# Expert stage of a two-layer decoder step: token rows stand still in four column groups, weights move

## What is computed

```python
g_sel = jnp.argmax(g_logit, axis=-1)                 # 1 group of 4
top_p, top_i = lax.top_k(jax.nn.softmax(e_logit, axis=-1), TOP_K)   # 2 experts of 8 in it
...
def expert_block(args):
    xb, e = args
    hid = jax.nn.silu(xb @ w_eg[e]) * (xb @ w_eu[e])   # 1024 -> 256, twice
    return hid @ w_ed[e]                               # 256 -> 1024
...
y = jnp.einsum('nkd,nk->nd', y_slot, gates)
```

## Time and profile before

| | us |
|---|---|
| median of three runs | 2886.36 |
| lowest, highest of the three | 2873.0, 2890.05 |
| span of the profiled execution | 2865.1 |
| expert blocks, first layer: first matmul to last | 1019.97 to 1387.8 |
| TensorE busy | 2605.3 (91%) |
| DMA over the span | 135 GB/s mean |

### The profile page before, as it was taken

One profiled execution on the slowest core, in us unless ns is written; L12 is line 12 of the kernel. 1 busy time (PEld: TensorE's weight loads), 2 busy tenths in 40 slices (PEclk: granted clock), 3 DMA queues, 4 the chain that ended last, 5 costly groups with the idle time before them and its releaser, 6 DMA issues.

```text
span 2865.1 us, 38998 instructions
## 1 busy us (share of the span) xinstructions
PE 2605.3 (91%) x15964; PEld 1817.8 (63%) x15964; DVE 1176.1 (41%) x2208; ACT 720.4 (25%) x1448; POOL 413.7 (14%) x561
## 2 busy tenths in 40 slices
PE   7999988899999889999699999888899997999994
PEld 5645556556667578887465455565666765888872
DVE  4155557543223433233351555584323334333225
ACT  1124453331003301111311244443211222111113
POOL 0004225110000011111100123251000000111111
PEclk9999998898999989999799999989999997999996
DMA  4001001342141268898410100113223214888954
GB/s 162 17 17 32 5 5 34 115 184 74 37 163 68 105 233 324 321 339 329 180 54 4 38 11 8 34 39 151 111 89 127 82 45 175 294 330 329 331 205 184
DMA packets 76932, 385.65 MB, mean 135 GB/s; under 512 B 25086, under 2 KB 31868, under 8 KB 65724
## 3 DMA queue, kind: packets, MB, share of 16 engines
q1 hardware_dynamic: 53164, 304.90, 29.2%
q0 software_dynamic: 23040, 76.59, 7.6%
q10 hardware_dynamic: 576, 2.10, 0.2%
HBM read 355.55 MB, written 44.55 MB: 140 GB/s over the span
## 4 chain that ended last, share of the span: by engine, by line
PE 73%; DVE 10%; PEld 4%; ACT 4%; issue 4%; DMA 2%; POOLq 1%; POOL 1%; PEldq 1%; SPq 0%; DVEq 0%; ACTq 0%
PE ps L1319 16%; PE ps L667 12%; PE ps L1332 8%; PE ps L1237 4%; PE ps L725 4%; PE ps L805 4%; PEld ps L667 4%; PE ps L817 2%; PE ps L833 2%; PE ps L1003 2%; PE ps L1308 2%; PE ps L783 2%; DVE arena L1993 1%; DVE nmax L1894 1%; PE ps L936 1%
## 5 line engine op out<-in xcount | busy, mean ns | idle before, releaser
L667 PE MATMUL ps<-arena,ring 128*128 128x352 f32 x1704 | 508.4, 461 | 3.4 <-DVE arena L1783 2.4
L1319 PEld LDWEIGHTS ps<-arena 128*128 128x128 f32 x4096 | 470.8, 193 | 35.7 <-issue 35.7
L1319 PE MATMUL ps<-arena 128*128 128x104 f32 x4096 | 470.5, 276 | 4.9 <-issue 2.5
L667 PEld LDWEIGHTS ps<-arena,ring 128*128 128x128 f32 x1704 | 324.8, 191 | 184.9 <-issue 5.7
L1332 PE MATMUL ps<-arena 128*104 128x512 f32 x512 | 230.4, 593 | 2.6 <-ACT arena L1713 2.6
L1713 ACT ACTIVATE arena<-ps 104x1024 f32<-104x1024 f32 x64 | 65.5, 1023 | 470.7 <-PE ps L1332 470.7
L2419 DVE TENSOR_SCALAR arena<-arena 128x208 f32<-128x208 f32 x64 | 17.2, 269 | 401.2 <-ACT arena L1706 401.2
L2554 POOL DMA_INDIRECT arena<-xrow,arena x64 | 70.5, 1102 | 671.7 <-PE ps L1308 353.9
L1332 PEld LDWEIGHTS ps<-arena 128*104 128x104 f32 x512 | 81.9, 170 | 104.0 <-issue 104.0
L805 PE MATMUL ps<-arena 96*128 96x512 f32 (+3 forms) x384 | 147.1, 493 | 0.0
L1481 ACT ACTIVATE ring<-ps 128x512 f32<-128x512 f32 (+2 forms) x192 | 87.3, 490 | 127.2 <-PE ps L817 127.1
(11 more groups left out here) (411 smaller groups left out, 3587.5 us busy)
## 6 DMA issues: line engine op xcount, KB each, us to landing
arena<-in_w_e SPq DMA_DIRECT2D x64, 3072.0 KB, 13.5
ring<-in_ring SPq DMA_DIRECT2D x56, 512.0 KB, 3.6
arena<-yrow SPq DMA_DIRECT2D x16, 1024.0 KB, 7.7
arena<-in_mem_k SPq DMA_DIRECT2D x16, 512.0 KB, 7.1
arena<-in_mem_v SPq DMA_DIRECT2D x16, 512.0 KB, 10.4
xrow<-arena SPq DMA_DIRECT2D x16, 512.0 KB, 6.3
x<-in_x SPq DMA_DIRECT2D x3, 1408.0 KB, 11.5
out_y<-arena SPq DMA_DIRECT2D x3, 1408.0 KB, 5.6
```

Source lines behind the costliest of these rows:

```text
L667: mm = pe.matmul(ps[:, (j % 2) * NCH + c, 0:CH], ring[:, j // per, (j % per) * units + k, :], src[:, k, tok], start=k == k0, stop=k == uni ...
L1319: mm = pe.matmul((gate_ps if m < 2 else up_ps)[:, m % 2, 0:rows], w_e[j][:, at:at + P], xb_t[:, p, k, 0:rows], start=k == 0, stop=k == KT - 1)
```

## The change

All of it concerns the expert stage.

1. A block has 128 rows and no longer belongs to one expert. `CAP` is 96 rows (three groups of 32), so 32 experts x 96 rows fill `NB` = 24 blocks. Each 32-row group of a block has its own expert: block 0 has experts 0, 0, 0, 1; block 1 has 1, 1, 2, 2; block 2 has 2, 3, 3, 3; and so on with a period of three blocks and four experts.
2. `gate_up` takes the rows as stationary operand, 32 at a time, and moves 512 weight columns (gate and up together) past them; the four groups write four 32-partition strips of one PSUM bank. It waits for the weights of *all* experts of its block before its first matmul.
3. The hidden values now come out with the row on the partition. A new step `turn_h` (two transposes) and a new copy by ScalarE, `keep_h`, turn them for `down`. `down` uses four 32-row groups as well.
4. `hidden` works on 128x256 in one bank of PSUM, after `take_x` of the next block instead of before it.
5. The weight slots are still four. Expert `e` is loaded when `down` of the last block that uses expert `e - 4` is over.
6. Loops are written out: 24 blocks, and up to `OVER` = 24 overflow blocks, each behind its own `If`, instead of a hardware loop over four.

```diff
-CAP = 104
-OVER = 20
-NBLK = NE + OVER
+CAP = 96
+GRP = 32
+NB = NE * CAP // P
+OVER = 24
+NBLK = NB + OVER
...
+        def experts_of(n):
+            return [(n * P + GRP * g) // CAP for g in range(P // GRP)]
+        def last_block(e):
+            return (CAP * (e + 1) - 1) // P
...
-                        sp.wait_ge(dn_done, n + 1)
-                        sp.sem_inc(turn, 1)
-                        load_w(j, n + 4)
+                for e in range(4, NE):
+                    sp.wait_ge(dn_done, last_block(e - 4) + 1)
+                    load_w(e % 4, e)
...
-                    pe.wait_ge(we_full[j], full)
+                    for e in sorted(set(experts)):
+                        pe.wait_ge(we_full[e % 4], 16 * loads(e))
                     pe.wait_ge(tx_evac, n + 1)
-                    pe.wait_ge(h_ready, n)
-                    for m in range(4):
-                        for k in range(KT):
-                            at = k * 512 + m * P
-                            mm = pe.matmul((gate_ps if m < 2 else up_ps)[:, m % 2, 0:rows], w_e[j][:, at:at + P], xb_t[:, p, k, 0:rows],
-                                           start=k == 0, stop=k == KT - 1)
+                    if n >= 2:
+                        pe.wait_ge(h_ready, n - 1)
+                    for k in range(KT):
+                        for g, e in enumerate(experts):
+                            r = slice(GRP * g, GRP * (g + 1))
+                            mm = pe.matmul(ps[r, 2 + n % 2, :], xb_t[:, n % 2, k, r], w_e[e % 4][:, k * 512:(k + 1) * 512],
+                                           start=k == 0, stop=k == KT - 1, skip_group_check=True)
...
+                def turn_h(n):
+                    pe.wait_ge(h_ready, n + 1)
+                    if n >= 1:
+                        pe.wait_ge(ht_evac, n)
+                    for m in range(2):
+                        mm = pe.transpose(ps[:, 6, m * P:(m + 1) * P], h_e[:, n % 2, m * P:(m + 1) * P], ident)
+                    mm.then_inc(ht_done, 1)
...
+                            for g, e in enumerate(experts):
+                                r = slice(GRP * g, GRP * (g + 1))
+                                mm = pe.matmul(ps[r, 4 + f, :], h_t[:, k, r], w_e[e % 4][:, at:at + 512],
+                                               start=k == 0, stop=k == 1, skip_group_check=True)
...
+                turn_x(0)
+                for n in range(NB):
+                    gate_up(n, experts_of(n), loads_of)
+                    if n >= 1:
+                        turn_h(n - 1)
+                    if n + 1 < NB:
+                        turn_x(n + 1)
+                    if n >= 1:
+                        down(n - 1, experts_of(n - 1))
+                turn_h(NB - 1)
+                down(NB - 1, experts_of(NB - 1))
...
+                    for o in range(OVER):
+                        with pe.If(n_over > o):
+                            n, experts = NB + o, [o % 4] * (P // GRP)
...
+                def keep_h(n):
+                    act.wait_ge(ht_done, n + 1)
+                    act.activation(h_t.rearrange("p m t -> p (m t)"), ps[:, 6, 0:2 * P], ACT.Copy).then_inc(ht_evac, 1)
...
+                take_x(0)
+                for n in range(NB):
+                    if n + 1 < NB:
+                        take_x(n + 1)
+                    hidden(n)
```

More of the change, by code:

```diff
@@ L1333, in down @@
                     mm.then_inc(dn_done, 1)
[L1335 to L1348, removed]
@@ L1349, in _, with loads_of @@
-                for n in range(NE - 3, NE):
-                    block(n, n % 4, n // 4, (n + 1) % 4, (n + 1) // 4, more=n < NE - 1)
-                down(NE - 1, 1, 3)
+                def loads_of(e):
+                    return e // 4 + 1
+                turn_x(0)
[5 more added lines that the diff above has]
+                        turn_x(n + 1)
+                    if n >= 1:
+                        down(n - 1, experts_of(n - 1))
@@ L1352, in _ @@
+                turn_h(NB - 1)
+                down(NB - 1, experts_of(NB - 1))
                 n_over = pe.value_load(over_i[0:1, 0:1], min_val=0, max_val=OVER)
                 with pe.If(n_over > 0):
[L1354 to L1360, removed]
+                    for o in range(OVER):
+                        with pe.If(n_over > o):
+                            n, experts = NB + o, [o % 4] * (P // GRP)
+                            turn_x(n)
+                            gate_up(n, experts, lambda e: NE // 4 + o // 4 + 1)
+                            turn_h(n)
+                            down(n, experts)
@@ L1718, in _ @@
[L1718 to L1723, removed]
-                    gate_exp(n)
-                    keep_y(n - 1, (n - 1) % 2)
-                keep_y(NE - 1, 1)
-                act.wait_ge(y_out, NE)
+                for n in range(NB):
+                    gate_exp(n)
+                    if n >= 1:
+                        keep_h(n - 1)
+                        keep_y(n - 1)
@@ L1728, in _ @@
+                keep_h(NB - 1)
+                keep_y(NB - 1)
+                act.wait_ge(y_out, NB)
                 n_over = act.value_load(over_i[0:1, 0:1], min_val=0, max_val=OVER)
                 with act.If(n_over > 0):
[L1730 to L1737, removed]
+                    for o in range(OVER):
+                        with act.If(n_over > o):
+                            n = NB + o
+                            gate_exp(n)
+                            keep_h(n)
+                            keep_y(n)
+                            act.wait_ge(y_out, n + 3)
+                            act.sem_inc(turn, 1)
@@ L2362, in _ @@
                 step(dve.tensor_tensor(jump, oend, nov, ALU.subtract))
[L2363 to L2364 removed]
+                step(dve.tensor_scalar(jump, jump, float(P), float(P * NB - CAP), ALU.mult, ALU.add))
+                step(dve.tensor_tensor(jump, jump, base, ALU.subtract))
                 dve.wait_ge(ranked, 2)
@@ L2574, in _ @@
                 stage_end(pool, 9)
-                for n in range(NE):
-                    if n + 2 < NE:
+                for n in range(NB):
+                    if n + 2 < NB:
                         pool.wait_ge(tx_done, n + 1)
```

116 lines of the change are left out of this document (48 added, 68 removed).

## The result

The changed kernel takes 3191.45 us (median of four runs; the kernel before 2887.11 beside it): 1.108 times the time before, 95% interval 1.105 to 1.112.

A forecast was written before the change was run, and what follows sets the result against it. TensorE was taken to bound the kernel, with late weights stalling it after the change. Span 2865.1 + 279 (expert stages) + 33 (overflow block) + 15 (jumps) = 3192, plus 21.3 to the median: 3213 us, range 3110 to 3330.

The forecast's parts named there:

- TensorE bounds the stage and DMA is close behind: Expert stages before the change: TensorE busy 100.00 of 100 us, 11.27 us an expert; DMA engines at 0.91.
- rival 4: Expert stage: weights are there in time, the DMA engines bound the stage, 2852 us; chance 3%.
- Four groups side by side: `gate_up` and `down`: four 32-column groups share the array; 7.0 and 3.5 us, a block of 128 rows 11.9 us.
- Which blocks stall: Expert stage: blocks 3, 4, 6, 7, ... 21, 22 wait for a weight load's whole landing, 14 a layer.
- What a stall costs: Each wait for weights in the expert stage: landing 12.0 us, issue 0.4, low clock 2.3, together 14.7 us.
- Until the last regular `down`: Expert stage up to its last regular `down`: 139.5 us more a layer, 279 for both.
- Overflow: End of the first layer's expert stage: one expert with 100 rows makes one overflow block, about 33 us.
- Jumps: The other 23 overflow bodies, jumped over by every engine: some 0.7 us each on TensorE, 15 us taken in all.
- The sum: Whole kernel's span: 2865.1 + 279 + 33 + 15 = 3192 us.
- From span to time: Whole kernel: the median of the runs lies 21.3 us above the span, giving 3213 us, 11% slower.
- The signs: Profile after: 28 gaps of 10 to 12 us put down to `in_w_e`, DMA share some 0.65, first stage 48 us longer.

The follow-up runs named there:

- The cut loads: Changed kernel with each expert's load cut in two, gate and up part asked for after `gate_up`, down part after `down`: 2811.11 us, ratio 0.977 to the kernel before.
- the run with filled gaps: Changed kernel with 12 idle f32 matmuls on TensorE before each of the 28 `gate_up`s that wait for weights: 3141.32 us.

## Why the prediction was right, point by point

Predicted 3213 us, range 3110 to 3330; measured 3191.45. The mechanism held: 28 stalls at the blocks named, the clock, one overflow block, slower jumps. That the number came so close is in part luck, as the points on the sum and on the span show.

- *TensorE bounds the stage and DMA is close behind.* The first half is confirmed. The second was wrong: "330 / 0.91 = 363 GB/s" took the busy share for a measure of what the DMA engines can still give. The cut loads run at 417 GB/s and 1.01. So the price of rival 4, 2852 us, was mis-sized; where weights are there in time the kernel takes 2811.
- *Four groups side by side.* `gate_up` is 6.98 us from its start to the next instruction (1113.37 to 1120.35), 0.436 a wave, `down` 3.45; I took 7.0 and 3.5. The Trainium skill's rule ("TensorE: Matmul & The Clock Gate", Part 3: Packing small matmuls), that weight loads overlap running matmuls only where the row group differs, would by my estimate have given 0.54 a wave; the trace does not agree with it here. A block is 11.68 us for the 11.9 I took: a block changes between full and grouped form twice, not four times, and the 0.3 us I took for that and for `keep_h` was near nothing.
- *Which blocks stall.* 3, 4, 6, 7, ... as worked out from the last block of each slot.
- *What a stall costs.* I took 12.4 for landing and issue and 2.3 for the clock, 14.7. A period takes 63.0 us on average, 35.0 of them work, so a stall is 14.0. The gaps are 11.7 us on average and the `gate_up` behind them is 2.0 us longer; the run with filled gaps gives 1.8 to 2.0 for the clock. The landing was over-estimated a little: 11.4 us on average, close to the "alone" figure of rows 7, where I took 12.0.
- *Until the last regular `down`.* Predicted 139.5 a layer. The first layer's ended 117.9 later than before (1505.67 for 1387.8); measured from the stage's start the layers lost 120.6 and 122.8. Some 0.7 us a stall (20 for both layers) and 0.2 us a block (10) make most of the difference; the rest is the start of the stage, where in the first layer expert 1's weights were there 4 us earlier than I took.
- *Overflow.* 33 us predicted, 30.4 measured for the block.
- *Jumps.* "Some 0.7 is its own ... I take 15": this term was mis-sized. It measured 44.8 in the time, 49.9 in the stage. The step that failed is the reading of rows 12: I put most of the 3.4 to 3.7 us down to matmuls still running. The branch did begin 2.8 us before they ended, but the overlap was not what made it long: with nothing running the median is 3.1 all the same.
- *The sum.* 279 + 33 + 15 = 327 against 330.0 in the profiled spans. It is that near because errors cancel: the way to the last `down` 36 too high, the overflow block 3 too high, the jumps 35 too low, and 7 us outside the stages that I did not foresee. Those 7 are within what executions of one kernel differ by (2863.9 to 2886.9 us in 15 runs of the kernel before).
- *From span to time.* I added 21.3 us, the distance of the median from the profiled span before. It does not carry over: of the changed kernel the median lies 3.7 *under* the span. This term alone is about all of the 21.6 us between 3213 and 3191.45, and by the medians the change cost 304 us where I forecast 327.
- *The signs.* The DMA share came down to 0.61 and 0.64 as said (0.65). The first stage is 77.6 us longer than the second, not 48, which is the jumps again. The gaps were not put down to the load of `in_w_e` but to "issue", and only the landings showed whose they are.

## What to carry to other kernels

Where a buffer's slot serves units that no longer match the units of work, list for each slot the last use that frees it and the first use of what comes next, in the order of the engine that waits: if the two stand next to each other, the whole landing is on the path, however empty the DMA engines are. Free a slot in the parts in which it is read, and ask for each part as soon as it is free. Written-out conditional code was not free on TensorE when it was skipped (2.8 to 3.5 us for 19 of 23 bodies here): put rare bodies behind one outer condition. And a forecast of a time should start from medians of runs; one profiled span can lie 20 us to the side.

## What the runs showed of the hardware that was not expected

- A taken branch of TensorE's sequencer costs 3.1 us (median of 23) over 106 matmul and transpose records and 0.20 us over 2; on VectorE, ScalarE and GpSimd, whose bodies are a few instructions, about 0.05. Each of the 19 long ones (2.8 to 3.5 us) had a 16 KB packet on the instruction queue, the 4 short ones (0.2 to 0.4 us) had none.
- The DMA busy share is no fixed measure of GB/s: 0.91 stood beside 330 GB/s with whole loads of 3072 KB in the kernel before, 1.01 beside 417 with pieces of 2048 and 1024 KB and more of them under way. What sets the ratio was not tried by itself; the same pieces asked for at the old moment made no load land sooner.
- Halving a load from 3072 to 1536 KB shortened its landing from 11.4 to 7.2 us (average of the 28 that TensorE waited for), not to half.
- Behind a pause of 6.98 us the clock was granted at 0.50 in the next 3 us, behind one of 1.67 us (cut loads, at 1274.78) `gate_up` ran at full clock (7.07 us); filling 28 pauses of 11.7 us with useless matmuls won 50 us.
